# A feed-forward in seven block products: one activation sum and one block exchange memory, two weight buffers exchange roles

## What is computed

```
D_MODEL = 1024
SEQ = 512
D_FF = 4 * D_MODEL
...
        hid = jax.nn.relu(rmsnorm(h, norm_mlp_g[i]) @ w_ff1[i])
        h = h + (hid * hid) @ w_ff2[i]
        gate = jax.nn.sigmoid(rmsnorm(h, ple_norm_g[i]) @ w_ple_gate[i])
        h = h + gate * (p[i] @ w_ple_proj[i])
    return rmsnorm(h, final_norm_g)
```

## Time and profile before

| What | us |
|---|---|
| median of 3 runs, with lowest and highest | 748.88 (748.5 to 749.48) |
| the profiled execution, its own time | 751.16 |
| its span, first to last instruction | 749.4 |
| PE busy in the span | 728.0 (97%) |
| DVE busy | 528.3 (71%) |
| ACT busy | 410.8 (55%) |
| POOL busy | 134.0 (18%) |
| granted TensorE clock, mean | 0.993 |

### The profile page before, as it was taken

How to read it: one execution, slowest core, us unless ns; L and a number is a source line. 1 busy time by engine, 2 the same in 40 slices (tenths; PEclk the granted TensorE clock), 3 DMA queues, 4 the chain that set the end, 5 groups by cost and what they waited for, 6 DMA issues and landing times.

```text
span 749.4 us, 9989 instructions
## 1 busy us (share of the span) xinstructions
PE 728.0 (97%) x3972; PEld 624.5 (83%) x3972; DVE 528.3 (71%) x553; ACT 410.8 (55%) x521; POOL 134.0 (18%) x112
## 2 busy tenths in 40 slices
PE   7999999999999999999999899989999999999996
PEld 7888877878878888888999689978999789978784
DVE  5546794576667465556787976879487956799774
ACT  5534456644674833315764733675356726483875
POOL 1021000766455000000102211122102220220000
PEclk9999999999999999999999999999999999999998
DMA  9633222342241163137839988789959896987311
GB/s 334 185 105 85 84 85 87 129 152 85 88 162 61 57 217 120 57 113 197 225 115 211 207 231 168 207 169 264 217 176 205 200 258 163 216 182 270 112 57 57
DMA packets 53381, 118.24 MB, mean 158 GB/s; under 512 B 5052, under 2 KB 6744, under 8 KB 53336
## 3 DMA queue, kind: packets, MB, share of 16 engines
q1 hardware_dynamic: 40968, 84.03, 34.5%
q0 software_dynamic: 11136, 29.36, 21.5%
q10 hardware_dynamic: 1232, 4.23, 1.8%
HBM read 96.60 MB, written 4.23 MB: 135 GB/s over the span
## 4 chain that ended last, share of the span: by engine, by line
PE 59%; DVE 16%; DMA 13%; issue 7%; ACT 4%; POOL 1%; DVEq 0%; ACTq 0%; SPq 0%; POOLq 0%
PE acc L1645 17%; PE acc L1647 16%; PE acc L1646 16%; DMA quarter<-in_w_ff 8%; DVE ring_lo L1403 7%; DMA quarter<-quarter 4%; PE side L1710 3%; DVE h L1498 2%; PE side L1807 2%; DVE fS_lo L1481 2%; ACT ring_hi L762 2%; DVE fA_lo L1481 1%; PE side L1774 1%; DVE fA_raw L1459 1%; PE side L1814 1%
## 5 line engine op out<-in xcount | busy, mean ns | idle before, releaser
L1403 DVE TENSOR_TENSOR ring_lo<-quarter,ring_hi 128x1024 fp32r<-128x1024 f32 x112 | 132.9, 1220 | 64.0 <-ACT ring_hi L762 64.0
L762 ACT ACTIVATE ring_hi<-quarter 128x1024 fp32r<-128x1024 f32 x112 | 113.7, 1050 | 99.5 <-DMA quarter<-in_w_ff 52.6
L1645 PE MATMUL acc<-w_hi,a_hi 128*128 128x512 f32 x256 | 104.4, 408 | 0.0
L1647 PE MATMUL acc<-w_hi,a_lo 128*128 128x512 f32 x256 | 100.1, 391 | 0.0
L1646 PE MATMUL acc<-w_lo,a_hi 128*128 128x512 f32 x256 | 99.7, 390 | 0.0
L642 POOL DMA_DIRECT2D quarter<-in_w_ff x24 | 29.2, 1219 | 265.0 <-DMA quarter<-in_w_ff 264.8
L1646 PE MATMUL acc<-xS_lo,ring_hi 128*128 128x256 f32 x256 | 72.4, 283 | 0.0
L1100 DVE TENSOR_TENSOR w_lo<-w_raw,w_hi 128x1024 fp32r<-128x1024 f32 x36 | 48.1, 1338 | 28.1 <-ACT w_hi L663 27.8
L1645 PEld LDWEIGHTS acc<-w_hi,a_hi 128*128 128x128 f32 x256 | 48.1, 188 | 10.8 <-issue 1.4
L1646 PEld LDWEIGHTS acc<-w_lo,a_hi 128*128 128x128 f32 x256 | 48.2, 188 | 10.7 <-issue 1.4
L1647 PEld LDWEIGHTS acc<-w_hi,a_lo 128*128 128x128 f32 x256 | 48.0, 188 | 10.4
(11 more groups left out here) (274 smaller groups left out, 1825.2 us busy)
## 6 DMA issues: line engine op xcount, KB each, us to landing
quarter<-in_w_ff SPq DMA_DIRECT2D x72, 512.0 KB, 5.0
w_raw<-in_w_in SPq DMA_DIRECT2D x36, 512.0 KB, 3.7
quarter<-quarter POOLq DMA_DIRECT2D x32, 512.0 KB, 5.2
quarter<-in_w_ff POOLq DMA_DIRECT2D x24, 512.0 KB, 9.8
w_raw<-in_w_out SPq DMA_DIRECT2D x16, 512.0 KB, 3.4
h<-in_x SPq DMA_DIRECT2D x8, 512.0 KB, 4.4
seg<-cs_dram ACTq DMA_DIRECT2D x8, 512.0 KB, 3.9
w_raw<-in_w_ple_gate SPq DMA_DIRECT2D x8, 512.0 KB, 4.5
```

Source lines behind the costliest of these rows:

```text
L762: act.activation(ring[n % 3][0][at], quarter[i][at], ACT.Copy).then_inc(form_hi, 1)
L1403: dve.tensor_tensor(lo[at], src, hi[at].bitcast(F32), ALU.subtract).then_inc(form_lo, 1)
L1645: pe.matmul(dst, st[0], mv[0], start=start, stop=False)
L1647: return pe.matmul(dst, st[1], mv[0], start=False, stop=stop)
```

## The change

The memory of S2 and of A12 is exchanged: A11 now shares both parts with A12, and S2 shares its hi part with S1; S2's raw sum and lo part have their region alone. So the sum S2 is moved ahead of `both(9)` on DVE, and S2's hi part ahead of A12's on ACT; A12's parts now wait for product B11 (which reads A11), S1's hi part for product T2 in place of B21. In the second matrix buffers 0 and 1 exchange roles: a function `home` puts B12, T3 and T1 in buffer m and B11 and T2 in buffer 1 - m. B12 is then loaded first and B11 after B21, and the next unit's B12 ahead of its B11. In every unit `both(5)` and U3 come before A11's lo part. In unit 0 the two additions on `h` stand after `both(9)`. At the end the last gain vector waits for product B21 in place of T2, and of the gate's weights the first two pieces wait for T4's sum.

The diff, cut:

```diff
-QUARTER = {"T3": 0, "T1": 0, "B12": 0, "B11": 1, "T2": 1, "B21": 2, "T4": 2, "B22": 3}
+
+
+def home(m, name):
+
+    return {"B12": m, "T3": m, "T1": m, "B11": 1 - m, "T2": 1 - m, "B21": 2, "T4": 2, "B22": 3}[name]
+
+
+LOADS = ((("B12", 0), ("B11", 1)), (("B11", 0), ("B12", 1)), (("B21", 0), ("B21", 1)), (("B22", 0), ("B22", 1)))
+SUMMED = ((("T3", 0), ("T2", 1)), (("T2", 0), ("T3", 1), ("T1", 1)), (("T4", 0), ("T4", 1)))
+RELOAD = 1
...
-        with ExitStack() as early:
-            f_lo["A11"] = sb("fA11_lo", [P, 4, 256], F32R, where=early)
+        f_lo["A11"] = f_lo["A12"] = sb("fA11_A12_lo", [P, 4, 256], F32R)
         f_raw["S2"], f_lo["S2"] = raw_lo("fS2")
-        f_lo["A12"] = sb("fA12_lo", [P, 4, 256], F32R)
...
-        f_hi["A11"] = f_hi["S2"] = sb("fA11_S2_hi", [P, 4, 256], F32R)
-        f_hi["A12"] = f_hi["S1"] = sb("fA12_S1_hi", [P, 4, 256], F32R)
+        f_hi["A11"] = f_hi["A12"] = sb("fA11_A12_hi", [P, 4, 256], F32R)
+        f_hi["S2"] = f_hi["S1"] = sb("fS2_S1_hi", [P, 4, 256], F32R)
...
-        HI_ORDER = ("A11", "S3", "A12", "S2", "S4", "A22", "S1")
+        HI_ORDER = ("A11", "S3", "S2", "S4", "A12", "A22", "S1")
...
-                i = QUARTER[name]
+                i = home(m, name)
                 row, col = int(name[1]) - 1, int(name[2]) - 1
                 for p in range(2):
                     if m:
-                        last_use = {"B12": "T1", "B11": "T2", "B22": "B22", "B21": "T4"}[name]
+                        last_use = ("T1", "T2", "T4", "B22")[i]
                         sp.wait_ge(form_lo, form_count(u, 0, last_use, p))
-                        if name == "B11":
+                        if i == 1:
                             sum_landed(sp, u, 0, "T4", p)
                             sp.wait_ge(t1_made, 2 * u + p + 1)
                     elif u:
-                        last_use = {"B12": "T1", "B11": "T2", "B22": "B22", "B21": "T4"}[name]
+                        last_use = ("T2", "T1", "T4", "B22")[i]
                         sp.wait_ge(form_lo, form_count(u - 1, 1, last_use, p))
-                        if name == "B11":
+                        if i == 0:
                             sum_landed(sp, u - 1, 1, "T4", p)
...
+                load_quarter(u, 1, "B12")
+                load_quarter(u, 1, "B21")
                 load_quarter(u, 1, "B11")
-                load_quarter(u, 1, "B21")
-                load_quarter(u, 1, "B12")
                 load_quarter(u, 1, "B22")
                 reload_b12(u)
                 if u < UNITS - 1:
+                    load_quarter(u + 1, 0, "B12")
                     load_quarter(u + 1, 0, "B11")
-                    load_quarter(u + 1, 0, "B12")
                     load_quarter(u + 1, 0, "B22")
                     load_quarter(u + 1, 0, "B21")
...
-            sp.wait_ge(ff_step, product_end(last, 1, "T2"))
+            sp.wait_ge(ff_step, product_end(last, 1, "B21"))
             load_gain(a["final_norm_g"], 0)
             for p in range(4):
-                sp.wait_ge(form_lo, form_count(last, 1, "T1" if p < 2 else "T2", 1))
-                if p >= 2:
+                sp.wait_ge(form_lo, form_count(last, 1, "T2" if p < 2 else "T1", 1))
+                if p < 2:
                     for i in range(2):
                         sum_landed(sp, last, 1, "T4", i)
...
-                    src = quarter[1][at]
-                pool.dma_start(quarter[QUARTER[name]][at], src, accum_op=ALU.add
-                               ).then_inc(t_landed[QUARTER[name]][p], 16)
+                    src = quarter[home(m, "T2")][at]
+                pool.dma_start(quarter[home(m, name)][at], src, accum_op=ALU.add
+                               ).then_inc(t_landed[home(m, name)][p], 16)
...
+                    elif name == "A12":
+                        act.wait_ge(ff_step, product_end(u, 1, "B11"))
+                        act.wait_ge(hid_lo, lo_count(u, "A11"))
                 else:
                     act.wait_ge(s_raw, s_count(u, name))
-                    if name == "S2":
-                        act.wait_ge(ff_step, product_end(u, 1, "B11"))
-                        act.wait_ge(hid_lo, lo_count(u, "A11"))
-                    elif name == "S1":
-                        act.wait_ge(ff_step, product_end(u, 1, "B21"))
-                        act.wait_ge(hid_lo, lo_count(u, "A12"))
+                    if name == "S1":
+                        act.wait_ge(ff_step, product_end(u, 1, "T2"))
+                        act.wait_ge(hid_lo, lo_count(u, "S2"))
                     elif name == "S4":
...
                 hidden(u, "A12")
-                split_a(u, "A12")
                 split_a(u, "S2")
                 both(10)
                 split_a(u, "S4")
+                split_a(u, "A12")
                 both(11)
                 split_a(u, "A22")
                 both(12)
...
-                    dve.wait_ge(ff_step, product_end(u, 1, "B11"))
...
+                both(5)
+                combine(u, "U3")
                 split_a(u, "A11")
-                both(5)
+                both(6)
                 if u == 0:
                     x_split("S4")
-                combine(u, "U3")
-                both(6)
                 combine(u, "C21")
                 both(7)
                 s_add(u, "S3")
@@ -1557,20 +1563,20 @@
                 split_a(u, "S3")
                 combine(u, "C12")
                 s_add(u, "S1")
+                s_add(u, "S2")
                 both(9)
-                s_add(u, "S2")
-                s_add(u, "S4")
-                split_a(u, "S2")
-                both(10)
-                split_a(u, "A12")
                 if u == 0:
                     dve.wait_ge(xn_ready, 2 * NS)
                     dve.tensor_tensor(h21, h21, h22, ALU.add).then_inc(h_added, 1)
                     dve.tensor_tensor(h12, h12, h22, ALU.subtract).then_inc(h_added, 1)
+                s_add(u, "S4")
+                split_a(u, "S2")
+                both(10)
                 h_add(u, "T3 right")
                 h_add(u, "T3 above")
+                split_a(u, "A12")
+                split_a(u, "S4")
                 both(11)
-                split_a(u, "S4")
                 h_add(u, "T2")
```

More of the change, by code:

```diff
@@ L357, in quarter_count @@
         def quarter_count(u, m, name):
-            if name == "B12":
-                return 16 * (3 * u + m + 1)
-            return 16 * (2 * u + m + 1)
+            i = home(m, name)
+            per_unit = len(LOADS[i]) + (i == RELOAD)
+            return 16 * (per_unit * u + LOADS[i].index((name, m)) + 1)
         def sum_landed(eng, u, m, name, p):
-            n = 3 * u + {"T3": m + 1, "T1": 3}[name] if QUARTER[name] == 0 else 2 * u + m + 1
-            eng.wait_ge(t_landed[QUARTER[name]][p], 16 * n)
+            i = home(m, name)
+            eng.wait_ge(t_landed[i][p], 16 * (len(SUMMED[i]) * u + SUMMED[i].index((name, m)) + 1))
         def pair(i):
@@ L517, in reload_b12 @@
                     k = 8 * u + 2 * p
-                    sp.dma_start(quarter[0][:, 2 * p:2 * p + 2, :], w_ff2[:, k:k + 2, 512:1024]
-                                 ).then_inc(q_landed[0][p], 16)
+                    sp.dma_start(quarter[RELOAD][:, 2 * p:2 * p + 2, :], w_ff2[:, k:k + 2, 512:1024]
+                                 ).then_inc(q_landed[RELOAD][p], 16)
             load_quarter(0, 0, "B12")
@@ L624, in t_add @@
                 if name == "T3":
-                    pool.wait_ge(q_landed[0][p], quarter_count(u, m, "B12"))
+                    pool.wait_ge(q_landed[home(m, "B12")][p], quarter_count(u, m, "B12"))
                     if m:
@@ L632, in t_add @@
                     pool.wait_ge(form_lo, form_count(u, m, "B11", p))
-                    src = quarter[0][at]
+                    src = quarter[home(m, "T3")][at]
                 elif name == "T1":
-                    pool.wait_ge(q_landed[0][p], 16 * (3 * u + 3))
+                    pool.wait_ge(q_landed[RELOAD][p], 16 * (3 * u + 3))
                     k = 8 * u + 2 * p
```

2 lines of the change are left out of this document (1 added, 1 removed).

## The result

The changed kernel takes **751.26 us** (median of 12 runs, 747.78 to 756.07), the kernel before, run beside it, 748.41 (12 runs, 746.99 to 749.6). The ratio is 1.004, with the interval 1.0023 to 1.0056: slower by 0.4%, where 736.8 and faster was forecast. The profiled execution took 752.46 us with a span of 750.6 and a mean granted clock of 0.989, against 751.16, 749.4 and 0.993.

What follows compares the result with a forecast made beforehand. TensorE was taken as the bound, busy 320.08 of 330 us, so gains come from its pauses and clock. 5.1 (unit 0) + 7.0 (units 1 to 3) = 12.1 us off 748.88 gives 736.8; 8-in-10 range 735.0 to 742.5.

Steps and rivals of the forecast that it cites:

- the second matrix: Units 1 to 3: the waits at T2 and B21 go, gaining 2.85 + 2.13 + 2.06 = 7.0 us.
- The place that it called decisive: Landing of B11's second half in the second matrix: needed by 484.0, forecast at 483.5 or 481.5, no cost taken.
- its sum over the two queues: B11's load beside T3's additions: 0.125 MB/us each until 480, then 0.35, so B11 is in at 483.5.
- Rival 1: B11 of the second matrix lands a little late; T2 waits in units 1 to 3: 743.4 us, chance 0.25.
- unit 0: First unit: B21 begins near 424.1 in place of 429.21, an idle of 1.0 us left at T2; gain 5.1 us.
- the reason given for the clock: Unit 0 at T2: idle shorter than the 2.24 us after which the clock stayed up, so 1.6 us loss gone.
- The same swap also brings forward T3's sum of the first matrix and with it T2, T1 and this whole half by up to 2 us: First matrix: T3's buffer is free at T2's last use, so B11's landing becomes 481.5 instead of 483.5.
- Steps of unchanged number (forms, loads, sums) cost as before: Whole kernel: forms, loads and sums whose number stays the same were given no added cost.
- the forecast's term: Unit 1: the loss at T2 and B21 goes, 2.85 us gained.
- Rival 2: B11's second half takes 12.4 us in units 1 to 3, T2 waits 4.6: slower, 756.6 us, chance 0.07.
- the order alone: If B11 or T3's sum is late, the new order by itself gives only 0.4 us a unit.
- the equal shares that the prediction worked with: POOL's and SP's queues beside T3's additions: 0.125 MB/us each while both run.

Runs made afterwards that it cites:

- experiment 1: The changed kernel with B21 loaded ahead of B22 for the next unit on SP: 740.64 us, ratio to the kernel before 0.9894.
- experiment 3: The changed kernel with VectorE's addition of T4 to h ahead of both(15) instead of behind it: 747.01 us, ratio to the kernel before 0.9974.
- experiment 2: The changed kernel with POOL's T2 additions of the first matrix held until B21's second half has landed (units 1 to 3): 751.30 us.
- Experiment 4: The changed kernel without the swap of buffers 0 and 1, SP's loads as in the kernel before; memory exchange and new orders kept: 745.56 us.
- experiment 6: The kernel before with B21 loaded ahead of B22 for the next unit: 752.17 us, ratio to the unedited kernel before 1.0053.
- experiment 5: The kernel before with only the swap of buffers 0 and 1, SP and POOL following; memory and ScalarE and VectorE orders unchanged: 749.24 us.
- experiment 10: The changed kernel with only unit 0's two h additions moved up behind C11's combine, loads as in the change: 747.41 us.
- experiment 7: The changed kernel with B21 loaded ahead of B22 for the next unit and unit 0's two h additions moved behind C11's combine: 738.96 us.

## Why the prediction was wrong

*Right: the second matrix.* T2's waits in units 1 to 3 are gone, and so are B21's behind them. The prediction had S2's lo part done at 500.0 if the two sums end at 488.36; in the changed kernel they end at 489.8 and it is done at 501.4, ten steps in 11.7 us as worked out, and PE does not wait. The place that it called decisive held: B11's second half was forecast to land at 481.5 to 483.5, and landed at 474.43 + 6.86 = 481.29. That this number fits is luck: the forecast had T3's additions beside that load until 480, but they had landed at 474.20, before it left, so its sum over the two queues was not put to the test in unit 1. In unit 2 they did meet (549.40 + 11.31 = 560.71 against a load from 554.36), the load took 9.11 us, and PE still did not wait. Rival 1 plays no part in the change itself (in experiment 1, where PE comes earlier, that load takes 9.1 us, and waits of 0.78 and 0.38 show).

*Right: unit 0.* Forecast an idle of 1.0 and no fall of the clock: 1.30 and 1.00. The gain up to unit 1's first matmul was forecast at 5.1 and is 5.04. But the reason given for the clock, a stop shorter than one after which it had stayed up, does not hold as a rule: it fell after 1.47 us in experiment 3 and after 1.86 in experiment 2. That it stayed up here is in part luck.

*Wrong: the price of the swap at its other end.* The step is the sentence "The same swap also brings forward T3's sum of the first matrix and with it T2, T1 and this whole half by up to 2 us", which counts the earlier additions as a help, together with "Steps of unchanged number (forms, loads, sums) cost as before". The additions do leave earlier, T3's by 9.4 us where PE is 5.0 earlier, and that puts them onto the loads ahead of B21's for the next unit, and T2's onto B21's own. Its 12.4, 11.0 and 9.7 us became 16.6, 14.6 and 17.3. I followed the loads of the second matrix through the queues, and never did the same for the four loads of the next unit, though the diff reorders them. (That SP loads into buffers 1, 2, 0, 3 in both kernels, as said under the change, is so for the second matrix alone. For the next unit it was 1, 0, 3, 2 and is 0, 1, 3, 2, so B12 lands, and T3's sum can leave, at 431.0 instead of 441.4.)

The account closes. Between the first matmuls of units 1 and 2 the kernel before takes 532.43 - 451.06 = 81.37 us and the changed one 530.89 - 446.02 = 84.87: 3.5 more. By steps that is 2.85 won at T2 and B21 (the forecast's term), 3.65 and a restart of 0.2 lost at the start, and 2.5 by the clock: 3.5. From unit 2 to 3 it is 80.69 against 79.39, 1.3 won: 2.13 less 0.72 and a restart of 0.15. In unit 3, 2.06 are won and 3.74 and 0.2 lost, and for the clock some 2.2 (25 matmuls in the 5.42 us from 619.93 on, where 25 x 0.12 = 3.0 would do, less the restart): 4.1 net. In all 5.04 - 3.5 + 1.3 - 4.1 = -1.3, and the profiled executions differ by 752.46 - 751.16 = 1.3.

*Rival 2* was right in kind and in size, at the wrong place. It named a single load stretched to 12.4 us beside T3's additions and let it hit B11. That row is B21's own second half going into unit 1, so the load on which the kernel broke stood among the quoted rows. What was not looked at is who waits for it: it landed 0.6 us before it would have cost PE anything.

*Also mis-sized:* the order alone, "0.4 a unit". Experiment 4 has 2.8 us for it in all, T2's waits in units 1 and 3 among it.

*On the queues*, the rows first. Over the whole stretch from 443 to 449 us POOL's queue and SP's move 0.84 and 0.81 MB, but at its edges one of the two hardly runs (POOL's moves 0.09 MB in the first us, SP's 0.02 in the last). Between 444 and 446 both run throughout (packets, MB, share):

```profile
q0 software_dynamic: 81, 0.33, 82.8%
q1 hardware_dynamic: 86, 0.16, 24.6%
```

The packets come out equal, and the bytes two to one for POOL: a packet of T2's sum, from one buffer to another, has about 4 KB (0.33 MB in 81), one of a load about 2 KB. For T3's sum the packets are of one size, and the bytes come out equal too. The prediction leaned on the Trainium skill, DMA: Bandwidth & Descriptors, section Queues, rings and completion order, where engines take turns between queues packet by packet; the trace agrees, with 81 packets against 86. So beside T2's sum a load gets a third of the bytes and not half, and the equal shares that the prediction worked with hold only beside T3's.

## What to carry to other kernels

When a change lets some transfers start earlier, list every transfer that is in flight in the time they move into, and for each one the slack of whoever waits for it; the loads for the next iteration count. A single number per boundary (here: B21 may land 2.4 us after the unit's first matmul) gives the wait of every one of these kernels in which the order behind the landing is the same, once the landing is known, and can be read from the trace of before; the landing cannot, since it hangs on what else is in flight. Where a stage ends earlier and a load's issue moves along with it, what is left to check is the load's duration, and the cheapest remedy is the order of the loads: first the one that is wanted first, if that one really is being waited for (experiments 1 and 6 are the same edit with opposite signs).

## What was not expected of the hardware

A load of 512 KB took 3.5 us at its shortest and 18.6 at its longest in these kernels; the load was of the same size and kind each time, what else was in flight was not.

The length of a stop of PE does not alone decide over the clock. It had fallen to its lower level after stops of 1.47 us (experiment 3, 0.50 between 536.4 and 539.7), 1.83 (experiment 6, 0.50 between 420.7 and 424), 1.86 (experiment 2), 2.53 (kernel before, the second of the earlier trace rows) and 2.83 (experiment 5, 0.55 between 532.8 and 536), and after all longer ones; it stayed at the upper level after 1.80 (experiment 3), 2.06 (experiment 6), 2.24 (kernel before) and 2.46 (experiment 10). What else decides these runs do not show. Where it was worked out, a fall cost another 1.6 us (kernel before) to 2.5 us (the change). The kernels with such waits also scatter most: 747.78 to 756.07 for the change, 742.11 to 750.5 in experiment 10, both over 12 runs, against 737.42 to 740.49 in the 6 of experiment 7. In the change the scatter goes with the clock: its mean was 0.993 to 0.996 in the four fastest runs and 0.986 to 0.989 in the five slowest. Whether the clock makes the scatter, or longer waits make both, was not tested. The Trainium skill, TensorE: Matmul & The Clock Gate, section HAM oscillation — how this bites in real kernels, describes this pattern, waits for transfers that let the clock fall again and again; units 1 and 3 of the changed kernel agree with it, with waits of 3.65 and 3.74 us and a granted clock of 0.50 behind both.
